# A two-layer hybrid encoder trunk on one core: the DMA turns of the feed-forward issued from ScalarE's queue, and ScalarE's chunk loop written out

## What is computed

```python
def _swiglu(h, w_gate, w_up, w_down):
    return (jax.nn.silu(h @ w_gate) * (h @ w_up)) @ w_down

# D_MODEL = 1024, D_FF = 2816, DEPTH = 2
x = x + 0.5 * _swiglu(_rms_norm(x, ffn1_norm[l]), ffn1_w_gate[l], ffn1_w_up[l], ffn1_w_down[l])
```

## Time and profile before

| | |
|---|---|
| median of 3 runs | 1064.58 us (1063.89 to 1068.48) |
| the profiled execution | 1062.78 us |
| its span | 1060.9 us |
| PE busy | 1048.6 us, 99% |
| ACT busy | 560.1 us, 53% |
| DVE busy | 673.2 us, 63% |
| POOL busy | 229.5 us, 22% |
| granted clock of PE | 1.0 of full speed throughout |
| DMA, SP's queue | 200.78 MB, 61.3% of the 16 engines' time |
| DMA, ACT's queue | 3.69 MB, 1.2% |

### The profile page before, as it was taken

One profiled execution on the slowest core, in us unless ns is written; L12 is line 12 of the kernel. 1 busy time (PEld: TensorE's weight loads), 2 busy tenths in 40 slices (PEclk: granted clock), 3 DMA queues, 4 the chain that ended last, 5 costly groups with the idle time before them and its releaser, 6 DMA issues. The chain is left out here.

```text
span 1060.9 us, 13912 instructions
## 1 busy us (share of the span) xinstructions
PE 1048.6 (99%) x5100; PEld 878.8 (83%) x5100; DVE 673.2 (63%) x899; ACT 560.1 (53%) x732; POOL 229.5 (22%) x258
## 2 busy tenths in 40 slices
PE   8999999999999999999999999999999999999998
PEld 5888887998888888888888888879988887888887
DVE  6556556599976465565656546556999665564563
ACT  6445445575762554454455535536767535454461
POOL 1840000049850000000048000002589300000000
PEclk9999999999999999999999999999999999999999
DMA  8776786365645367767656686674366345867761
GB/s 277 220 230 202 211 242 225 127 219 169 208 149 179 95 203 218 225 200 219 217 159 204 186 249 204 206 247 157 132 209 232 105 159 129 220 203 220 225 203 48
DMA packets 176701, 205.06 MB, mean 193 GB/s; under 512 B 49264, under 2 KB 147856, under 8 KB 176656
## 3 DMA queue, kind: packets, MB, share of 16 engines
q1 hardware_dynamic: 174064, 200.78, 61.3%
q10 hardware_dynamic: 2592, 3.69, 1.2%
HBM read 192.90 MB, written 1.05 MB: 183 GB/s over the span
## 5 line engine op out<-in xcount | busy, mean ns | idle before, releaser
L1390 DVE TENSOR_TENSOR wlo<-raw,whi 128x2048 fp32r<-128x2048 f32 x154 | 351.4, 2286 | 69.1 <-ACT whi L1044 69.0
L604 PE MATMUL bank<-whi,hThi 128*128 128x512 f32 (+1 forms) x976 | 379.2, 388 | 0.3 <-DVE wlo L1390 0.3
L606 PE MATMUL bank<-whi,hTlo 128*128 128x512 f32 (+1 forms) x976 | 373.7, 383 | 0.0
L605 PE MATMUL bank<-wlo,hThi 128*128 128x512 f32 (+1 forms) x976 | 373.6, 383 | 0.0
L1044 ACT ACTIVATE whi<-raw 128x2048 fp32r<-128x2048 f32 x178 | 338.7, 1908 | 16.2 <-DMA raw<-in_ffn_w_up 7.9
L604 PEld LDWEIGHTS bank<-whi,hThi 128*128 128x128 f32 x976 | 183.4, 188 | 36.0 <-DVE wlo L1390 0.7
L606 PEld LDWEIGHTS bank<-whi,hTlo 128*128 128x128 f32 x976 | 183.2, 188 | 35.8
L605 PEld LDWEIGHTS bank<-wlo,hThi 128*128 128x128 f32 x976 | 183.5, 188 | 34.2
L1118 ACT ACTIVATE gThi<-vtok 128x512 fp32r<-128x512 f32 x40 | 25.3, 632 | 277.1 <-DVE vtok L1478 237.8
L604 PE MATMUL bank<-whi,gThi 128*128 128x512 f32 (+1 forms) x416 | 162.7, 391 | 2.7 <-DVE gTlo L1395 2.7
L605 PE MATMUL bank<-wlo,gThi 128*128 128x512 f32 (+1 forms) x416 | 161.2, 387 | 0.0
(11 more groups left out here) (163 smaller groups left out, 805.8 us busy)
## 6 DMA issues: line engine op xcount, KB each, us to landing
raw<-in_ffn_w_down SPq DMA_DIRECT2D x88, 512.0 KB, 5.4
raw<-in_ffn_w_gate SPq DMA_DIRECT2D x86, 512.0 KB, 4.2
raw<-in_ffn_w_up SPq DMA_DIRECT2D x86, 512.0 KB, 5.3
raw<-in_w_in SPq DMA_DIRECT2D x48, 512.0 KB, 4.9
raw<-in_w_out SPq DMA_DIRECT2D x16, 512.0 KB, 4.4
raw<-in_w_in SPq DMA_DIRECT2D x8, 544.0 KB, 7.6
raw<-in_w_mla_out SPq DMA_DIRECT2D x8, 512.0 KB, 3.9
raw<-in_w_conv_out SPq DMA_DIRECT2D x8, 512.0 KB, 4.8
```

The costliest lines, as they stand in the source:

```text
L604: nc.tensor.matmul(out, lh, rh, start=start, stop=False, skip_group_check=skip)
L605: nc.tensor.matmul(out, lh, rl, start=False, stop=False, skip_group_check=skip)
L606: return nc.tensor.matmul(out, ll, rh, start=False, stop=stop, skip_group_check=skip)
L1390: nc.vector.tensor_tensor(wlo[:, slot(u0, RING), 0:n], raw[:, slot(u0, RAW), 0:n], whi[:, slot(u0, RING), 0:n].bitcast(F32), ALU.subtract) ...
```

## The change

The forty turns are issued by ACT, each directly behind the second planes instruction of its chunk, and no longer by SP. They wait for the same semaphores. ACT's loop over steps 1 to 8 is written out, so that its waits are on constants. SP issues weights and the small loads alone. The parameters that served the loop's registers go.

```diff
-            def plane_turn(l, f, c):
-
-                sp.wait_ge(planes_ready, per_turn(l, f, c) * TT)
-                sp.wait_ge(joined, per_turn(l, f, c))
-                sp.dma_start_transpose(turned[:, :, :], planes.rearrange("p b k t f -> p (b k t f)")
-                                       ).then_inc(turned_landed, 16)
...
                     gate_up(l, f, c, c, 0)
                     gate_up(l, f, c, c, 1)
-                    if c > 1:
-                        plane_turn(l, f, c - 2)
                     down(l, f, c - 1, c - 1)
...
+                def plane_turn(c):
+
+                    act.wait_ge(planes_ready, per_turn(l, f, c) * TT)
+                    act.wait_ge(joined, per_turn(l, f, c))
+                    act.dma_start_transpose(turned[:, :, :], planes.rearrange("p b k t f -> p (b k t f)")
+                                            ).then_inc(turned_landed, 16)
...
                     split_planes(0, 1)
-
-                def pair(c, c0, i=0):
-                    u = UB[f] + 2 + 3 * c0
-                    round_joined(c - 1, c0 - 1)
-                    split(l, u, i)
+                    plane_turn(0)
+
+                def pair(c):
+                    u = UB[f] + 2 + 3 * c
+                    round_joined(c - 1, c - 1)
+                    split(l, u)
                     silu(c, 0)
-                    split(l, u + 1, i)
+                    split(l, u + 1)
                     split_planes(c, 0)
                     silu(c, 1)
-                    split(l, u + 2, i)
+                    split(l, u + 2)
                     split_planes(c, 1)
+                    plane_turn(c)
 
                 first()
-                with act.Fori(0, (NCH - 3) // 2) as i:
-                    pair(i * 2 + 1, 1, i * 2)
-                    pair(i * 2 + 2, 2, i * 2)
-                pair(NCH - 2, NCH - 2)
+                for c in range(1, NCH - 1):
+                    pair(c)
```

More of the change, by code:

```diff
@@ L398, in first @@
                         gate_up(l, f, 0, 0, 0)
-                        if f == 0:
-                            plane_turn(l - 1, 1, NCH - 2)
                         gate_up(l, f, 0, 0, 1)
@@ L429, in _ @@
                 for h in range(2):
-                    if h == 1:
-                        plane_turn(l, 0, NCH - 2)
                     block_of(l, UM + M_PR + h, a["w_in"], 4 * h * P, 4, O1, PR)
@@ L450, in _ @@
                 ffn(l, 1)
-            plane_turn(DEPTH - 1, 1, NCH - 2)
             sp.wait_ge(x_new, 6 * DEPTH + 1)
@@ L1038, in _, with split @@
         def _(act):
-            def split(l, u0, turns=0):
-                n = (l * (U_LAYER // RAW) + turns + (u0 // RAW + 1)) * 32
+            def split(l, u0):
+                n = (l * (U_LAYER // RAW) + (u0 // RAW + 1)) * 32
                 act.wait_ge(raw_landed[slot(u0, RAW)], n)
-                act.wait_ge(unit_free, l * U_LAYER + turns * RAW + (u0 + 1))
+                act.wait_ge(unit_free, l * U_LAYER + (u0 + 1))
                 nc.scalar.activation(whi[:, slot(u0, RING), 0:USED[u0]], raw[:, slot(u0, RAW), 0:USED[u0]],
```

## The result

| | median | runs |
|---|---|---|
| before | 1064.24 us (1060.25 to 1068.48) | 4 |
| after | 1110.05 us (1099.70 to 1116.15) | 4 |

The ratio is 1.0427, with an interval of 1.0396 to 1.0457: the change costs 46 us. The forecast was 1101.0 us, in a range of 1060 to 1128.

What follows compares the result with a forecast made beforehand. PE, busy 99%, was taken as the bound, with ScalarE's loop having 0.6 us to spare per chunk. Later turns add 27.5 us in chunks, 8.0 at first turns, 3.1 at chunk 9: +38.6 on 1062.78, 1101 us, range 1060 to 1128.

Steps and rivals of the forecast that it cites:

- the first turns: First turn of each feed-forward: three meet a nearly empty queue, so the down unit passes whole, 2.8 us; 8.0 us together.
- Who issues: Issuing turns from ACT instead of SP: nothing won, and the moved issue time falls where ACT would wait anyway; zero.
- The loop written out: ScalarE's loop without register instructions: join to next turn 9.37 us instead of 9.54, gain 0.17 a chunk, nothing on PE.
- The turn's place among the transfers: Two queues share row by row, so down rows delay each turn 1.6 us, landing 7.8 instead of 6.2; 27.5 us in chunks.
- 55 gate rows pass beside 55 turn rows: Per DMA engine, gate/up rows left when the turn starts alternate with its 64 rows; nothing lost, they went first anyway.
- third rival: Slower by more: the down unit passes whole each time, turn 9.0 us, total 1141 us; chance 0.13 including cases between.
- The turn of chunk 9 ahead of a mixer: Turn with w_in units on both sides: taken as unchanged on average near 8.5 us; 1.6 us, twice, 3.1.
- PE's clock unchanged: Sign that the forecast is right: PE's clock stays as before; no time was added for it.
- No change (1063): Queues share in long runs or the turn needs only its own work behind gate rows; PE stays bound, 1063 us; chance 0.30.
- faster (1058.5): Second rival: the turn passes the gate rows, landing after 3 to 4.5 us, PE's turn waits go, 1058.5 us; chance 0.10.
- The first rival: No change: the turn lands after 6.2 us or a little less, PE stays the bound, 1063 us; chance 0.30.
- The tells: Signs: median landing near 7.8 us and gTlo waits 30 to 40 us if right; below 6.9 and some 3 if wrong.

## Why the prediction was right, and where it was not

**The total and the mechanism.** Forecast 1101, measured 1110.05, inside the range; the profiled execution took 1099.7. The loss comes from the order between turn and weights that two queues no longer keep, which the runs with order restored show. That the profiled execution came out so near the sum was luck: its terms were off in opposite directions. PE's further waits and busy time split as follows: 13.6 us in chunks 1 to 8 (forecast 27.5), 1.5 at the first turns (forecast 8.0), 11.5 at chunk 9 (forecast 3.1), and 10.1 us of busy time, most of it the clock (forecast 0). The range, too, was wide enough to hold no change at all.

**Who issues.** Right. The turn is issued 0.03 us behind the planes, takes ACT 1.25 us, and no engine waits for that. At chunk 9 the issue took up to 3.6 us, still beside a longer turn.

**The loop written out.** Right. From the join of turn 4 to the issue of turn 5 it takes 9.37 us, and as much in the other steps:

```profile
106.33 0.75 DVE L1470 COPY vtok<-qkT 128x1024 uint16<-128x1024 uint16 x1 [7.21 <-DMA qkT<-qkT]
...
115.70 1.25 ACTq L1101 DMA_TRANSPOSE qkT<-qkT  x1
```

And it is worth nothing on PE: 0.9996.

**The turn's place among the transfers: the step that was mis-sized.** It said that the last 9 turn rows on each engine would let 9 down rows pass, 1.6 us in every turn, 7.8 us landing, and 32 x 0.86 + 8.0 = 35.5 us. What ran is not a uniform 7.8 but 6.4 us on average in 22 turns and 9.2 in ten; the mean of all is 7.29 against 6.25. The error lies in "when the turn can start, 1.2 us after its issue", and so in "55 gate rows pass beside 55 turn rows". The count of gate rows at 1.2 us was right (58 an engine in turn 5), but the turn's first row moved at 3.5 us, with 14 of them left. So the turn met down rows only if an engine still had turn rows when they came, and then that engine let all 16 pass, not 9: 16 x 0.17 = 2.7 us. That is the third rival's path and its condition (a start delayed by more than 1.2 us), shown row by row for five of the ten late turns; the other five land as late. A late turn of 9.0 us costs 9.37 + 9.0 - 16.32 = 2.05 us, the price that this rival gave for all 32. Nor do ten such turns cost 20.5: the other turns' loop takes 9.37 + 6.2 = 15.6 us and gains back 0.7 us of slack each. PE's waits for gTlo grew by 13.7 us, not 35.5. The first turns of the four feed-forwards, priced at 8.0 us with the down unit passing whole in three, landed after 7.4, 5.5, 5.0 and 6.2 us (5.5, 4.5, 5.0 and 6.4 before), and PE's waits there grew by 1.5 us.

**The turn of chunk 9 ahead of a mixer: the other mis-sized term.** It was taken as unchanged near 8.5 us, 3.1 us for two. It took 13.9 and 13.6 us. Before, SP issued two w_in transfers, then the turn, then four more, one behind another in one queue:

```profile
166.64 0.94 SPq L360 DMA_DIRECT2D raw<-in_w_in  x2
168.86 2.23 SPq L385 DMA_TRANSPOSE qkT<-qkT  x1
171.13 4.66 SPq L360 DMA_DIRECT2D raw<-in_w_in  x4
```

Now SP issues all six from 179.68 on, for 8.96 us on end, and the turn goes out on ACT's queue at 180.59:

```profile
179.68 8.96 SPq L360 DMA_DIRECT2D raw<-in_w_in  x6
```

The four later ones no longer stand behind it, and their rows share the DMA engines with its own. PE's waits for chunk 10's transposes grew by 12.9 us, those for gTlo at chunk 9 shrank by 1.4, and some 4 us of half clock came behind them. It was the place with the most weights in flight, and I priced it by an average.

**PE's clock unchanged.** Wrong. Two waits of 6 to 7 us and two of 2 to 3 us were followed by 1.2 GHz for a while, 7.0 us in all. The forecast spread its waits over the chunks at 0.9 us each, and so never asked what a long one would do.

**The rivals.** No change (1063) and faster (1058.5) are refuted by the 46 us of the first measurement and the 20 on chip 0. The first rival's landing was right for 22 of 32 turns, but not for its reason. The Trainium skill, "DMA: Bandwidth & Descriptors", section "Queues, rings and completion order", has an engine change queues after a whole packet of some 9 to 17 rows. The packet records of the late turns show otherwise: beside down rows the two queues alternate one by one, and on one engine in turn 5, three turn rows and two gate rows take turns. Here the measurement decides. The punctual turns were punctual because they had few or no down rows to share with: with the down unit held back altogether the slowest land after 6.3 us too.

**The tells.** The median landing, forecast at 7.8 with "below 6.9" as the sign of the first rival, read 6.3 and would have pointed to the wrong case. The PE waits for gTlo (16.4, forecast 30 to 40) pointed between the two. A median is no tell where the cause strikes some turns and not others.

**What stays open: which engine runs late.** In turns 2, 3, 5, 32 and 35 the late engine had 19 to 24 turn rows left, some 0.3 us of them at 0.014 us each, so little decides. In five late turns of the changed kernel's first profile (2, 11, 19, 21, 32) a 16 KB packet of the queue that loads instructions runs for 0.9 to 1.1 us, from 0.7 to 1.0 us after the issue; that it is on the late engine is not recorded. Three of these (11, 21, 32) are late in every profile in which down units of 4096-byte rows can pass (the two of the changed kernel, and the one with the turn of chunk 9 back), and slightly late even in before (6.4, 6.6, 6.8 us). With the order restored the same packets run beside them, and they land after 6.2 to 6.4 us. But turns 3, 4, 5, 24, 35 and 38 are late without such a packet. No run was made on this.

## What to carry to other kernels

A queue is also an ordering. Before moving a latency-critical transfer to another queue, list what is issued behind it on the old one within its landing time: these now compete with it. If it must move, move the follower along, or hold it with a wait for the landing; both cost nothing here. Price such a change at the busiest place, not at the average one, and read the landings one by one: 10 of 32 were late under an unchanged median. Leave a little slack in a loop that runs beside the bound engine. Here 0.6 us a chunk were enough for before and not for a turn 3 us late.

## What the runs showed of the hardware that was not expected

- A turn issued on ACT's queue 0.75 us after loads on SP's moved its first row 3.5 us after its issue, with most of their rows through, just as on SP's own queue (3.5 us in before). With nothing ahead it moved its first row after 1.2 us and needed 3.0 us for all. The second queue brought no earlier start.
- An engine with 22 turn rows of 256 bytes left let 16 down rows of 4096 bytes pass, one after each turn row: 0.3 us of its own rows took 2.8 us (5.54 to 8.37 in turn 5). Many small rows beside few large ones pay for the large ones.
- The same kernel lost 46 us in the first measurement and 20 on chip 0, while before differed by 5 (1064.24 and 1058.92). Where the loss hangs on one of 16 DMA engines being some 0.3 us behind, it may well differ so; that was not measured by itself.
- One late turn cost twice: 7.3 us of waiting, and 2.4 us of half clock behind it (turn 9, ahead of the first mixer).
